# Expert tokens beyond the wide 128 in groups of 32, with 32x32 blocks turned by VectorE

## The reference

```python
def swiglu(t, w_gate, w_up, w_down):
    return (jax.nn.silu(t @ w_gate) * (t @ w_up)) @ w_down

def moe_swiglu(h, w_router, w_gate, w_up, w_down):   # 8 experts, hidden width 3584
    t = h.reshape(256, 1024)
    top_val, top_idx = lax.top_k(t @ w_router, 2)
    gates = jax.nn.softmax(top_val, axis=-1)
    combine = jnp.sum(jax.nn.one_hot(top_idx, 8) * gates[..., None], axis=1)
    out = jnp.zeros_like(t)
    for e in range(8):
        out = out + combine[:, e:e + 1] * swiglu(t, w_gate[e], w_up[e], w_down[e])
    return out
```

## Time and profile before

| | us |
| --- | --- |
| median of 3 runs | 1340.64 |
| lowest and highest | 1339.22 and 1342.0 |
| the profiled execution, its own time | 1340.69 |
| its span in the trace | 1339.0 |
| stage of pair 0 | 430 to 650 |
| stage of pair 1 | 650 to 867 |
| stage of pair 2 | 867 to 1110 |
| stage of pair 3 | 1110 to 1324 |

### The profile page before, as it was taken

How to read it: one execution, slowest core, us unless ns; L and a number is a source line. 1 busy time by engine, 2 the same in 40 slices (tenths; PEclk the granted TensorE clock), 3 DMA queues, 4 the chain that set the end, 5 groups by cost and what they waited for, 6 DMA issues and landing times.

```text
span 1339.0 us, 20505 instructions
## 1 busy us (share of the span) xinstructions
PE 1287.6 (96%) x8949; PEld 804.7 (60%) x8949; DVE 554.4 (41%) x806; ACT 441.6 (33%) x660; POOL 10.8 (1%) x35
## 2 busy tenths in 40 slices
PE   7999999998998999999799999999999999999997
PEld 6787788877787665768657476633333354333343
DVE  5585555546586574644757465310000001200003
ACT  6564444436553463533536355200000000000001
POOL 3000000000000000000000000000000000000000
PEclk9999999999998999999999999999999999999999
DMA  9235544264004999999999999999999999999991
GB/s 351 108 135 206 216 186 183 89 241 172 18 0 190 419 420 402 420 365 414 404 394 384 402 421 417 417 420 420 419 384 359 360 357 355 388 377 407 418 415 57
DMA packets 129067, 418.75 MB, mean 313 GB/s; under 512 B 4248, under 2 KB 8384, under 8 KB 128976
## 3 DMA queue, kind: packets, MB, share of 16 engines
q1 hardware_dynamic: 127872, 416.30, 78.9%
q0 software_dynamic: 544, 1.12, 0.3%
q10 hardware_dynamic: 560, 0.01, 0.0%
HBM read 416.37 MB, written 1.05 MB: 312 GB/s over the span
## 4 chain that ended last, share of the span: by engine, by line
PE 87%; DVE 5%; ACT 3%; DMA 3%; issue 1%; ACTq 0%; SPq 0%; DVEq 0%
PE bank L2066 27%; PE bank L2137 14%; PE bank L1705 14%; PE bank L1706 13%; PE bank L1707 13%; DMA ring<-in_moe_w_down 3%; PE bank L2002 2%; PE bank L1996 2%; PE bank L2085 1%; ACT raw_d L782 1%; DVE lo L1090 1%; DVE mx L1180 1%; DVE raw_d L1177 1%; DVE w_lo L1524 1%; ACT hi L716 1%
## 5 line engine op out<-in xcount | busy, mean ns | idle before, releaser
L1524 DVE TENSOR_TENSOR w_lo<-ring,w_hi 128x1024 fp32r<-128x1024 f32 x168 | 201.9, 1224 | 62.7 <-ACT w_hi L716 55.1
L2066 PE MATMUL bank<-ring,late_acts 128*32 128x256 f32 (+3 forms) x1936 | 215.8, 434 | 0.0
L716 ACT ACTIVATE w_hi<-ring 128x1024 fp32r<-128x1024 f32 x168 | 174.9, 1059 | 93.2 <-PE bank L1707 77.4
L1705 PE MATMUL bank<-hi,act_hi 128*128 128x512 f32 (+1 forms) x400 | 157.0, 392 | 10.3 <-DVE lo L1090 6.6
L2066 PEld LDWEIGHTS bank<-ring,late_acts 128*32 128x32 f32 (+1 forms) x1936 | 85.7, 120 | 121.5 <-issue 100.8
L2137 PE MATMUL bank<-ring,at_buf 128*32 128x256 f32 (+1 forms) x1408 | 157.1, 450 | 0.5 <-ACT at_buf L716 0.5
L716 ACT ACTIVATE at_buf<-bank 128x256 f32<-128x256 f32 (+2 forms) x40 | 18.0, 449 | 414.4 <-PE bank L2085 414.4
L1707 PE MATMUL bank<-hi,act_lo 128*128 128x512 f32 (+1 forms) x400 | 153.9, 385 | 0.0
L1706 PE MATMUL bank<-lo,act_hi 128*128 128x512 f32 (+1 forms) x400 | 153.9, 385 | 0.0
L1546 DVE TENSOR_TENSOR silu_buf<-silu_buf,bank 128x512 f32<-128x512 f32 (+2 forms) x56 | 29.4, 536 | 227.5 <-PE bank L2066 194.1
L1090 DVE TENSOR_TENSOR lo<-raw_gu,hi 128x1024 fp32r<-128x1024 f32 x96 | 112.3, 1221 | 24.4 <-ACT hi L716 23.6
(11 more groups left out here) (240 smaller groups left out, 1255.5 us busy)
## 6 DMA issues: line engine op xcount, KB each, us to landing
ring<-in_moe_w_up SPq DMA_DIRECT2D x50, 2048.0 KB, 14.3
ring<-in_moe_w_down SPq DMA_DIRECT2D x49, 2048.0 KB, 13.6
ring<-in_moe_w_gate SPq DMA_DIRECT2D x48, 2048.0 KB, 13.0
raw_gu<-in_w_in SPq DMA_DIRECT2D x7, 2048.0 KB, 12.3
ring_after<-in_moe_w_gate SPq DMA_DIRECT2D x7, 2048.0 KB, 9.7
ring_after<-in_moe_w_down SPq DMA_DIRECT2D x7, 2048.0 KB, 12.0
ring_after<-in_moe_w_up SPq DMA_DIRECT2D x6, 2048.0 KB, 14.3
raw_gu<-in_dense_w_gate SPq DMA_DIRECT2D x5, 2048.0 KB, 7.9
```

The costliest lines, as they stand in the source:

```text
L716: return nc.scalar.activation(out, in_, ACT.Copy, **kw)
L1524: v.tensor_tensor(w_lo[:, n % WP, :], flat(u)[:, q * 1024:(q + 1) * 1024], w_hi[:, n % WP, :], ALU.subtract).then_inc(w_lo_done, 1)
L1705: mm(out, ah, wh, start=start, stop=False, **kw)
L2066: ins = mm(bank[b][c * g.n:(c + 1) * g.n, 0:width], acts[STEPS[s][0]][:, k, g.col:g.col + g.n], by_rows(u, n)[:, kl, c * width:(c + 1) * w ...
```

## The change

All of it lies in the branch experts_by_size and its tables.

- Non-wide tokens come in groups of 32 only: an expert of 96 places has three, one of 64 has two. Each product is 32x256, or 32x128 in a 512 block for gate and up.
- The turns of non-wide groups go from TensorE and ScalarE to VectorE, as 60 calls v.transpose in 32x32 blocks on silu_buf directly behind the gating product (small_at_done). For that the hidden columns have to lie otherwise in the gate and up sums, and so the moving operand of these products reads runs of 32 elements, 128 apart. 56 of the 161 transposes of 128x128 stay, for wide groups.
- In a unit that has both, the fp32 products come ahead of the wide ones, for gate, up and down. In the first up unit the small product waits for its silu before the wide ones start.
- The wait for a slot whose last unit was wide is now for w_lo_done, with unit_used where there are fp32 products too.
- The groups' places in the row tiles and sum banks are two tables, ROW_OF and SUM_OF. Pairs 0 and 2 fill one tile's 128 rows with both experts' groups; rows are added by 24 products in place of 32, and pairs 0 and 2 have one call of gates fewer. Groups share banks more often: 5 zero products (L2120) in place of 2.
- The last rows are copied out of their banks by ScalarE and VectorE together (first_sum_done, y_last).

The experts' branch has 4269 instructions of TensorE before and 6919 after.

```diff
 class Group:
...
-        self.n = 64 if self.full else 32
...
+        self.n = 64 if self.wide else 32
+        self.first_slot = self.n * i if self.wide or w == 1 else first + 32 * self.j
...
+        elif w == 0 and first > 0:
+            self.gate = self.up = 5
         else:
...
+            self.gate = (0, 5, 1)[i]
+            self.up = self.gate if cap > 32 else 1
+        self.acc, self.acc_col = SUM_OF[p, w, i]
+        self.tile, self.row = ROW_OF[p, w, i]
...
-                if BEFORE[u] >= 0:
-                    sp.wait_ge(unit_used, BEFORE[u] + 1)
+                b = BEFORE[u]
+                if b in FIRST_PIECE:
+                    sp.wait_ge(w_lo_done, FIRST_PIECE[b] + 4)
+                if b >= 0 and (UNIT_READ[b] or SLOT[u] != SLOT[b]):
+                    sp.wait_ge(unit_used, b + 1)
...
+                    for g in small_groups(s):
+                        v.transpose(e_at(s, g)[:, 0:n], e_silu(s, g)[:, 0:n]).then_inc(small_at_done, 1)
...
                 def products(s, what, i, n):
...
-                    if wide(s):
-                        wide_products(s, what, i, n)
-                    else:
-                        landed(u)
...
+                    if len(small) > 0:
+                        landed(u)
...
                     for g in small:
                         if what == "u" and i == 0 and g.up == g.gate:
                             pe.wait_ge(e_silu_done, summed(s, groups_of(s).index(g)))
...
-                            for c in range(m):
-                                ins = mm(bank[b][c * g.n:(c + 1) * g.n, 0:width],
-                                         acts[STEPS[s][0]][:, k, g.col:g.col + g.n],
-                                         by_rows(u, n)[:, kl, c * width:(c + 1) * width],
...
+                            w = by_rows(u, n)[:, kl, :].rearrange("p (t a j) -> p a t j", a=4, j=32)
+                            for c in range(4):
+                                ins = mm(bank[b][32 * c:32 * c + 32, 0:n // 4], acts[STEPS[s][0]][:, k, g.col:g.col + 32],
+                                         w[:, c], start=k == 0, stop=k == KT - 1)
...
+                    if wide(s):
+                        wide_products(s, what, i, n)
```

More of the change, by code:

```diff
@@ L172, in small_groups, with wide_groups @@
     return [g for g in groups_of(s) if not g.wide]
[L175 to L178 removed]
+def wide_groups(s):
+    return [g for g in groups_of(s) if g.wide]
 def tile_rows(p, tile):
@@ L221 @@
         N_UNITS += 1
+UNIT_READ = [len(small_groups(_s)) > 0 for _what, _s in UNIT_ORDER for _ in range(BLOCKS[STEPS[_s][2]][1] // 512)]
 LAST_WIDE = max(FIRST_PIECE)
@@ L937, in turned_out @@
                 def turned_out(s, j):
[L938 to L942, removed]
+                    n = BLOCKS[STEPS[s][2]][1] // 2
+                    act.wait_ge(turn_done, wide_turned(s, j))
+                    copy(at_wide_hi[:, j, 0:n], bank[2][:, 0:n]).then_inc(at_done, 1)
                 def hi_pieces(u, q0=0, q1=4):
@@ L967, in silu_of @@
                         act.wait_ge(gate_done, early(s, i))
-                    nc.scalar.activation(e_silu[g.buf][:, 0:n], bank[g.gate][:, 0:n], ACT.Silu).then_inc(e_silu_done, 1)
+                    if i == 0 and s > 0:
+                        act.wait_ge(small_at_done, SMALL_SUMS[s])
+                    nc.scalar.activation(e_silu(s, g)[:, 0:n], bank[g.gate][:, 0:n], ACT.Silu).then_inc(e_silu_done, 1)
                 m = pair_slots(0)
@@ L996, in experts_by_size @@
                     else:
-                        for j in range(min(2, len(before_))):
+                        for j in range(turns):
                             turned_out(s - 1, j)
@@ L1006, in experts_by_size, with last_rows_out @@
                             hi_pieces(u)
-                last = GROUPS[NP - 1, 1][0]
+                def last_rows_out(g):
+                    for c in range(2, 4):
+                        ins = copy(yt[g.row:g.row + 32, g.tile, c * 256:(c + 1) * 256],
+                                   bank[g.acc][32 * c:32 * c + 32, g.acc_col:g.acc_col + 256])
+                    return ins
+                act.wait_ge(unit_used, last_unit("d", NS - 2) + 1)
+                for g in GROUPS[NP - 1, 0]:
+                    ins = last_rows_out(g)
+                ins.then_inc(y_last, 1)
+                act.wait_ge(first_sum_done, 1)
+                last_rows_out(GROUPS[NP - 1, 1][0])
                 act.wait_ge(unit_used, N_UNITS)
-                copy(yt[last.row:last.row + 64, last.tile, 512:1024],
-                     bank[last.acc][64:128, :]).then_inc(y_last, 1)
+                last_rows_out(GROUPS[NP - 1, 1][1]).then_inc(y_last, 1)
             def experts_of_any_size():
@@ L1636, in experts_of_any_size @@
                                 .then_inc(all_gated_done, 1)
+                        u = last_unit("d", s - 1) if s > 0 else last_unit("u", s)
+                        pieces = 4 * sum(b in FIRST_PIECE and b > pieces_to for b in range(u + 1))
+                        pieces_to = u
+                        if pieces > 0:
+                            dve.wait_ge(unit_used, u + 1)
+                            v.tensor_copy(over[:, 0:1], over_any[:, :]).then_inc(w_lo_done, pieces)
             def last_norm():
@@ L2174, in experts_by_size @@
                     extra(p, 3 * i + 2)
-                pe.wait_ge(e_gated_done, SUMS[NS])
-                for j in range(len(groups_of(NS - 1))):
-                    turn(NS - 1, j)
                 down(NS - 1)
                 pe.wait_ge(y_out, 2 * NP - 1)
+                pe.wait_ge(y_last, 1)
                 pe.wait_ge(extra_out, EXTRA[NP - 1, 9])
```

201 lines of the change are left out of this document (100 added, 101 removed), and 10 rows, old and new, of tables (ROW_OF, SUM_OF).

## The result

The changed kernel takes 1323.03 us (median of 4 runs, 1321.06 to 1324.72) against 1341.32 of the kernel before in the same comparison: a ratio of 0.9865, with a 95% interval of 0.9845 to 0.9885. That is 18.3 us less where 35.7 was forecast. The profiled execution took 1323.9, with a span of 1322.1, 16.9 less than before. The time lies in the range of the prediction (1288 to 1324), at its slow end, and about half of the expected gain is missing.

What follows compares the result with a forecast made beforehand. The prediction took TensorE as the bound, with loads waiting for it. Its terms, +1.8, -5.8, -16.9 and -14.8 us for pairs 0 to 3, made -35.7 from 1340.6: 1305 us, range 1288 to 1324.

Steps and rivals of the forecast that it cites:

- Groups of 32: Units of 96-token experts take 5.20 us instead of 5.45: 10.5 us less in pair 2, 5.3 in pair 3.
- Transposes off TensorE: Turns of non-wide groups leave TensorE in all four pairs: together 17.0 us less.
- Shared row tiles: 24 products that add rows instead of 32: 4.2 us less in each of pairs 1 and 3.
- The silu wait: In pair 0's up units TensorE waits for the small group's silu, in four blocks: +9.1 us in all.
- The gating wait: In pair 0 the next step's wait for gatings loses the cover of the small products: +2.5 us.
- The w_lo waits of pair 0: Waits for low halves of weights; small products moved into four of them in down units give -6.7 us.
- Rival B: Each group of 32 pays for its start, 1.86 us: no gain or a little slower, 1340; chance 0.04.
- rival C: Pair 0 loses more, through waits and lower clock: 11 to 19 us of the gain go, 1316 to 1324; chance 0.15.
- That just holds: In pair 3 TensorE eats 21 us of the loads' lead of seven slots, up to 35, so the lead suffices.
- the floor of 1281: Earliest end the weight loads allow, 168 units at 420 GB/s, then the last products and tail: 1281 us.
- Rival A: Gate and up products slowed by reading weights in runs of 32, 128 apart: +183 us, 1488; chance 0.10.
- the estimate of 25 ns for each instruction: From the skill's 60 cycles per matmul: 2650 more instructions would cost 66 us, 1371; the prediction found its rows unsupportive.

Runs made afterwards that it cites:

- e1: Changed kernel with gate and up of 512 blocks joined in one instruction for experts without wide tokens, half the instructions there: 1316.16 us, ratio 0.9825.
- e3: Changed kernel with each load bringing only half of its unit from the ninth unit of pair 2 on: 1303.86 us.
- e8: Changed kernel with pair 0's small silu right behind its gate sum, and gate and up joined in 512 blocks of pairs 2 and 3: 1303.06 us, ratio 0.9722.
- e2: Changed kernel with gate and up products reading weights contiguous instead of in runs of 32, same instructions and bytes: 1323.8 us.
- e4: Changed kernel with every product of pair 2's second and third 1024 block cut in two, twice the instructions: 1391.74 us.
- e7: Changed kernel with the edits of both e4 and e3, doubled instructions and half loads: 1347.35 us.
- e9: e7 with loads of an eighth of their unit instead of half: 1311.96 us.

## Why the prediction was half right

- **Groups of 32: right.** 5.18 us a unit measured (1045.79 to 1056.15 for two), 5.20 forecast, 5.45 before. That is 1.73 a group, and there is no start to pay.
- **Transposes off TensorE: right.** None is left in pairs 2 and 3. VectorE's take 0.27 to 0.45 us, 0.40 in the middle (below), where the earlier trace rows gave 0.29 to 0.69; 60 are some 24 us of VectorE. Weight loads of down products waited 2.3 us for them in three places, and the products behind had no gap. The Trainium skill has such a transpose sustain one element per cycle and lane (Vector Engine (DVE) Microarchitecture Reference, The reshape front-end and per-opcode configuration). The trace can only be held against its slope: 128 more elements for each lane take 0.13 us more (0.40 against 0.27), about 1 ns each, and half of the 0.27 us does not grow with them; no run here gives the engine's cycle.

```profile
L1596 DVE STREAM_TRANSPOSE at_buf<-silu_buf x24: 268/403/446, 885.8 to 1283.3; 128x256 f32<-128x256 f32 x18, 128x128 f32<-128x128 f32 x6
...
  PEld bank L2184: 2.3, 3
```

- **Shared row tiles: right in pair 3, less in pair 1.** The section on the change put it wrongly: it is tile 1 that pairs 0 and 1 fill together (and 2 and 3), so that its rows are added once for two pairs. In pair 1 some of the products that went had covered waits: 0.8 us for the wide silu, and a w_lo wait of 2.0 in place of 1.33. Behind the longer wait the clock is 0.50 from 709.80 to 713.20, some 1.7 us, where it stayed at 1.00 behind the old one. I had left out that cover. With the gap of 1.9 us these are 5.1 us, about what pair 1 fell short of its -5.8.
- **The silu wait: right in kind, 1.3 us too high.** 7.8 us in four places against 9.1 forecast, the first 3.50 against 3.9. The gating wait is 1.7 + 0.5 against 2.5. The w_lo waits of pair 0 are gone entirely: of 15.3 us the 4.23 at the border to pair 1 and 1.33 inside it were not pair 0's, so 9.7, where I took 6.7. So pair 0 gained 2.8 where +1.8 was forecast, and pair 1 1.0 where -5.8 was: together -3.8 against -4.0. That the two agree is luck: pair 0 got 3.0 us more out of its w_lo waits than forecast, and pair 1 gave 4.8 less than its terms.

ScalarE and then TensorE in the second block of pair 0 (the second fence is TensorE's first up product):

```profile
506.50 1.08 ACT L1009 ACTIVATE silu_buf<-bank 128x512 f32<-128x512 f32 x2 [0.29 <-PE bank L1765]
507.47 1.06 ACT L757 ACTIVATE w_hi<-ring 128x1024 fp32r<-128x1024 f32 x1
508.42 0.39 ACT L1009 ACTIVATE silu_buf<-bank 128x256 f32<-128x256 f32 x1
```

```profile
508.95 1.93 PE L2122 MATMUL bank<-ring,first_acts 128*32 128x256 f32 x32 [2.48 <-ACT silu_buf L1009]
```

- **Rival B's dismissal: the step that failed.** The prediction put the 2650 more instructions at nothing. Its sum has no term for them, rival B prices them only as a time on TensorE, and the earlier trace rows, a second 32-token unit at half of a 64-token unit's time, set that price at nothing. As a time on TensorE this was right: a unit takes 5.18 us with 192 instructions and 5.24 with 384. What was left out is how fast instructions come. The rows are of a 1024 block, and there a unit of three groups of 32 needs one transfer in 6.9 us; in a 512 block it needs one in 3.5, and beside the loads they came 5.6 apart. Measured, that is 12.7 us of gaps in pairs 2 and 3, 1.9 in pair 1, and some 2.9 for the lower clock behind the two longest (0.49 of 2.65 us and 0.46 of 3.40): 17.5 us, and the forecast was 18 us too low. The stages give about the same: 8.2 + 3 in pair 2 (3 us is what the terms would have saved there), 4.6 + 2.2 in pair 3 and 1.9 in pair 1, 20 us. e1 takes all the gaps away by half the instructions, e3 all but 3.1 us in pairs 2 and 3 by half the loads.
- **What could have been seen.** The need, by a division: in the kernel before a unit of a 96-token expert is 96 instructions in 5.45 us in a 1024 block, and 192 in 5.5 in a 512 block, one transfer in 14.5 and in 7.3 us, and the change doubles both rates. The limit could not be seen, since no gap of this kind stands in the experts' stage before. So this was a rival to be named with a chance, and it was not named. That the time still fell into the range is luck: the slow end was drawn for rival C.
- **"That just holds": nearly.** The lead of the loads in pair 3 was right as long as the gaps were there. With them gone it is 5.7 us short (e1, e8): the step "that just holds" was too high by that. The time of e8 is 22 us above the floor of 1281: in pair 2 loads still wait for slots, since TensorE at 5.18 a unit is slower than they are.
- **Rival A** fell by e2. The Trainium skill's rule (SBUF — State Buffer, Door 1: The DMA port swizzle), by which the new pattern is free, agrees with e2; the stationary rows at stride 4 still speak against its edge. The Trainium skill's warning of cutting a small dimension (TensorEngine Tiling (Array Packing), Instruction Overhead) is borne out, though not by its mechanism: the estimate of 25 ns for each instruction didn't show (96 more product records in a unit take 0.06 us more), the fetching did.
- **Rival C** named the right time, 1316 to 1324, for the wrong place: pair 0 took 2.8 us less than before, where rival C had it lose 11 to 19 more than forecast.

## What to carry to other kernels

When an edit multiplies instructions, divide: instructions of the densest stretch by its time, against what the instruction transfers of the profile bring, and above all beside bulk loads. An average over the kernel hides it; here one block in four had twice the rate. A gap whose releaser is "issue", in the midst of a run of equal products, is the sign, and the same number of records between two such gaps is the proof. And a cover is worth naming on both sides: removing work in front of a wait that it hid gives less than its duration.

## What the runs showed of the hardware

- One transfer of 16 KB brings some 256 instructions, and TensorE needs one for each product record and one for each weight load. When they come too late, the gaps lie 128 product records or a multiple apart, and each ends 2.2 to 2.5 us after a transfer began (changed kernel, e4).
- With the instructions of pair 2's middle blocks doubled the transfers came 5.4 us apart in the mean under full weight loads (e4), 4.6 with loads of a half (e7), and 3.9 with loads of an eighth (e9), about as fast as TensorE asked; two units of e9 ran at one in 3.5 us.
- Products of 32x128 at 192 records a unit take 5.24 us, those of 32x256 at 96 take 5.18: half the columns at nearly no loss, as long as the instructions are there.
- Behind a gap of 2.52 us the granted clock was 0.51 over 2.65 us (changed kernel), behind one of 3.77 it was 0.60 over 3.0 (e8).
